# Two token sequences of 256 columns in the place of one of 512, with the adaLN products moved to TensorE

## What is computed

```python
for i in range(DEPTH):                      # h = x, hc = ctx, m / mc = adaln(c) / adaln(c_ctx), 9 rows of 1024 each
    h  = half_ffn(h,  m,  0, g[0], g[1], ffn_w_in[i, 0], ffn_w_out[i, 0])
    hc = half_ffn(hc, mc, 0, g[0], g[1], ffn_w_in[i, 0], ffn_w_out[i, 0])
    u, uc = modulated_norm(h, g[2], m, 3), modulated_norm(hc, g[2], mc, 3)
    y, yc = mixer(u, uc, ..., ctx_out=i < DEPTH - 1)     # x's queries see the keys of both, the context's only its own
    h = half_ffn(gated_residual(h, y, g[3], m, 3, 1.0), m, 6, ...)
    if ctx_out:
        hc = half_ffn(gated_residual(hc, yc, g[3], mc, 3, 1.0), mc, 6, ...)
```

## Time and profile before

| | |
|---|---|
| median of 3 runs | 2817.33 us (2813.98 to 2820.81) |
| span of the profiled execution, first to last instruction | 2814.7 us |
| busy: TensorE / its weight loads | 2602.5 / 2247.8 us |
| busy: VectorE / ScalarE | 1710.1 / 1002.3 us |
| read from HBM | 348.91 MB |
| mean granted TensorE clock | 0.928 of full |

### The profile page before, as it was taken

How to read it: one execution, slowest core, us unless ns; L and a number is a source line. 1 busy time by engine, 2 the same in 40 slices (tenths; PEclk the granted TensorE clock), 3 DMA queues, 4 the chain that set the end, 5 groups by cost and what they waited for, 6 DMA issues and landing times. The chain is left out here.

```text
span 2814.7 us, 39425 instructions
## 1 busy us (share of the span) xinstructions
PE 2602.5 (92%) x14572; PEld 2247.8 (80%) x14572; DVE 1710.1 (61%) x3265; ACT 1002.3 (36%) x1597; POOL 0.8 (0%) x5
## 2 busy tenths in 40 slices
PE   7989988888998999999987899999899999888997
PEld 7989978758997888877855678888688888667997
DVE  3365554446556888435666678873678863656555
ACT  4244442334443222233255332223322223335443
POOL 0000000000000000000000000000000000000000
PEclk9599997758999999998998999999899999989999
DMA  5245452103543554332310135533245532211443
GB/s 212 106 144 185 157 223 84 43 1 134 180 160 131 180 179 150 110 114 88 113 53 1 60 125 176 178 130 103 80 165 179 179 117 92 94 60 61 165 166 118
DMA packets 65732, 351.54 MB, mean 125 GB/s; under 512 B 7376, under 2 KB 10960, under 8 KB 40528
## 3 DMA queue, kind: packets, MB, share of 16 engines
q1 hardware_dynamic: 62272, 341.86, 34.6%
q10 hardware_dynamic: 3344, 8.12, 0.8%
HBM read 348.91 MB, written 1.05 MB: 124 GB/s over the span
## 5 line engine op out<-in xcount | busy, mean ns | idle before, releaser
L309 DVE TENSOR_TENSOR wlo<-raw,whi 128x2048 fp32r<-128x2048 f32 (+1 forms) x282 | 582.2, 2064 | 602.8 <-ACT whi L302 602.0
L314 PE MATMUL bank<-HN_hi,whi 128*128 128x256 f32 (+1 forms) x2976 | 645.1, 342 | 58.7 <-ACT HN_hi L826 31.8
L302 ACT ACTIVATE whi<-raw 128x2048 fp32r<-128x2048 f32 (+1 forms) x282 | 488.7, 1733 | 526.5 <-PE bank L314 508.3
L314 PE MATMUL bank<-HN_hi,wlo 128*128 128x256 f32 (+1 forms) x2976 | 626.6, 335 | 0.0
L314 PE MATMUL bank<-HN_lo,whi 128*128 128x256 f32 (+1 forms) x2976 | 606.3, 334 | 0.0
L314 PEld LDWEIGHTS bank<-HN_hi,whi 128*128 128x128 f32 x2976 | 485.3, 195 | 137.5 <-issue 33.7
L314 PEld LDWEIGHTS bank<-HN_hi,wlo 128*128 128x128 f32 x2976 | 485.6, 194 | 52.5 <-issue 0.5
L314 PEld LDWEIGHTS bank<-HN_lo,whi 128*128 128x128 f32 x2976 | 479.4, 194 | 53.9
L314 PE MATMUL bank<-G_hi,whi 128*128 128x256 f32 (+1 forms) x1056 | 207.4, 345 | 4.4 <-DVE wlo L309 4.4
L314 PE MATMUL bank<-G_lo,whi 128*128 128x256 f32 (+1 forms) x1056 | 198.9, 336 | 0.0
L314 PE MATMUL bank<-G_hi,wlo 128*128 128x256 f32 (+1 forms) x1056 | 198.6, 336 | 0.0
(11 more groups left out here) (223 smaller groups left out, 2086.5 us busy)
## 6 DMA issues: line engine op xcount, KB each, us to landing
raw<-w_main SPq DMA_DIRECT2D x186, 1024.0 KB, 4.8
raw<-w_down SPq DMA_DIRECT2D x96, 704.0 KB, 4.1
half<-w_ada SPq DMA_DIRECT2D x128, 512.0 KB, 4.4
raw<-w_ada SPq DMA_DIRECT2D x8, 1024.0 KB, 4.7
ARENA<-cmp_k_w ACTq DMA_DIRECT2D x1, 2048.0 KB, 11.4
ARENA<-cmp_v_w ACTq DMA_DIRECT2D x1, 2048.0 KB, 18.6
H<-x SPq DMA_DIRECT2D x1, 1024.0 KB, 6.7
H<-x ACTq DMA_DIRECT2D x1, 1024.0 KB, 6.1
```

The source lines that it names most:

```text
L302: NS.activation(WHI[n % 2][:, 0:size], RAW[slot][:, 0:size], ACT.Copy).then_inc(sems["w_hi"], 1)
L309: NV.tensor_tensor(WLO[slot][:, 0:size], RAW[slot][:, 0:size], WHI[n % 2][:, 0:size].bitcast(fp32), SUB)\
L314: return NT.matmul(out[:, 0:N], (WHI[n % 2], WLO[n % SLOTS])[w][:, k * wk + col:k * wk + col + P], x[xp][:, kx, 0:N], start=start, stop=stop)
```

## The change

Nearly all of `build` is rewritten. What it does:

- x and the context have tensors of their own (`Lane`), with 256 columns each. Every weight block of the 117 is loaded, split and multiplied once for x and once for the context.
- A plan of block uses in one order (`take`) replaces the loops; the program is fully unrolled. All weight blocks go through the four `RAW` slots, the 72 of adaLN and the 4 of the NSA compression too. `WHI` has three buffers.
- Three generators are interleaved when the program is written: x's sequence, the context's (`c`), adaLN's (`a`). x's yields `("L", us)` where it expects a wait of that length, `D` ahead of a block and `d` in its middle. In a wait (`fill`) the context gets half blocks at a price of 2.9 us each. Ahead of every second block of x (`pace`) one adaLN block is put in. `want` runs the context in one piece up to its keys and values.
- adaLN on TensorE: the weights are the moving side, 8 float32 matmuls of 256 columns, with 32 stationary columns in turn in four column tiles; then a ScalarE copy, two small matmuls and a VectorE add.
- Silu is formed as tanh on ScalarE and two multiplies on VectorE, over 512 columns (two tiles) at a time.
- The context's FFN is cut in three chunks of hidden features (8, 8, 6 tiles), and its down projection is summed over them in `YC` by VectorE. The context's attention has two banks and one unit in flight.
- The first mixer's parts and `od_in`'s blocks are in another order, so that the rotations, pooling and the compression stand between linear blocks.

By these budgets, counted over the yields of the new text: of the context's 117 blocks 29 are put into x's waits (8 in the NSA attention, 1 in the group norm after it, 5 in the first mixer and the norm after ev_out, 15 in the other norms of x and the tile norm after ga_in). 24 stand in one piece ahead of the first attention, with one norm of the context among them, and 64 ahead of the second, with two. The first 12 adaLN blocks stand in ev_in, 10 of these in a row.

```diff
+def modulation():
+    bank = BANK[5]
+    for b in range(72):
+        yield ("D",)
+        n = take("a", "w_ada", b, BLK, False)
+        landed(n)
+        if on(pe, silu_c if b == 0 else None, free.get(bank.name)):
+            for k in range(KD):
+                g = k % 4
+                mm = NT.matmul(bank[32 * g:32 * g + 32, 0:T], CCOL[:, k, :], RAW[n % SLOTS][:, k * T:(k + 1) * T],
+                               start=k < 4, stop=k >= 4, skip_group_check=True, tile_position=(0, 32 * g))
+            mm.then_inc(sems["block_done"], 1)
+        splits(n)
+        ...
+        if on(act, done(n), picked):
+            NS.activation(ROWS[:, :], bank[:, 0:T], ACT.Copy).then_inc(rows.sem, 1)
+        yield ("L", 0.5)
+        ...
+                mm = NT.matmul(bank[:, T + 2 * m:T + 2 * m + 2], ROWS[:, m * P:(m + 1) * P], vec("pick"), start=True, stop=True)
+def fill(us):
+    credit[0] = min(credit[0] + us, 6.0)
+    ...
+    while credit[0] > 0:
+        if ahead["c"] in ("D", "d"):
+            credit[0] -= 2.9
+            step("c")
+        elif ahead["c"] == "L" and "c" not in late:
+            late.add("c")
+            credit[0] -= 0.3
+            step("c")
+        ...
+def pace(kind):
+    ...
+    if kind == "D":
+        spent[0] += 1
+        if ahead["a"] == "L":
+            step("a")
+        if ahead["a"] == "D" and "a" not in paused and ((0, 1) not in gains_known or spent[0] % 2 == 0):
+            step("a")
+    ...
+    if ahead["c"] == "L":
+        step("c")
+def want(label):
+    while label not in passed:
+        step("c")
+def two_tiles(S, n, dsts, x, ks, start, stop, waits=None, signal=None, tiles=2):
+    landed(n)
+    for m in range(tiles):
+        mm = three(dsts[m], n, m * P, x, ks, start, stop, None if m else waits)
+        ...
+        if m == 0:
+            splits(n)
+        if m == 0 and tiles == 2:
+            opened[0] = S.tag
+            yield ("d",)
+        ...
+def norm(S, post, pre, ready, mod=()):
+    ...
+    if post:
+        yield ("L", 3.0)
+        tot_y = add_up(S, S.YY, sum_y, 0, now(f"{t}_sq_sum"), *ready)
+        ...
+        yield ("L", 1.0)
+        ...
+        yield ("L", 1.5)
+        ...
+    yield ("L", 3.0)
+    rs_h = spread_in(S.SQ[-1], S.wide_h, diag)
+    ...
```

In the context's FFN the last chunk of the down projection ends in `put_out`, which for each of 8 output tiles has 3 operations on ScalarE and 4 on VectorE with one buffer for the squares, and `linear` and `ffn` of the context wait for all 8 feature tiles of its norm:

```diff
+            dst = y if c == 1 else S.TMP[0][:, :]
+            ...
+                NV.tensor_tensor(dst, y, bank[:, :], ADD).then_inc(ev.sem, 1)
+            ...
+            if c == 2:
+                for m in range(2):
+                    held["tmp"] = put_out(S, S.TMP[0][:, m * T:(m + 1) * T], 2 * mp + m, gain, ev)
...
+    x = yield from norm(C, True, pre(C, 0, 1), [now("c_evac")], mods)
+    zk = yield from linear(C, "da_in", [(4 + b, 2 * b) for b in range(4)], KC, ready=x[1])
```

A unit of the context's attention issues its scores, maxima, exps and scalings in one step; the VectorE operations after the exps stand behind them in its queue, ahead of x's:

```diff
+            if on(dve, sc, o):
+                ...
+                NV.tensor_scalar(NEGM, MAXM, -scale, None, MUL).then_inc(ng.sem, 1)
+            if on(act, ng):
+                ...
+            if on(dve, ex):
+                NV.reciprocal(CO, SUM).then_inc(m1.sem, 1)
+                ...
+                NV.scalar_tensor_tensor(PB[:, 0, :], PB[:, 1, :], CO[:, 1:2], PB[:, 0, :], MUL, ADD).then_inc(m4.sem, 1)
+            yield ("L", 1.2)
```

More of the change, by code:

```diff
@@ L52 @@
[L52 to L81, removed]
@@ L84 @@
[L84 to L96, removed]
+SLOTS, HIS = 4, 3
@@ L100 @@
+GU = 22
+PAIRS = KF // 2
+CHUNKS = ((0, 8), (8, 16), (16, 22))
+MAIN, _at = {}, 0
+for _name, _n in [("ev_in", 6), ("ev_out", 4), ("gu0", GU), ("od_in", 14), ("od_out", 4), ("gu1", GU), ("gu2", GU),
+                  ("da_in", 12), ("da_out", 4), ("gu3", GU), ("gu4", GU), ("ga_in", 6), ("ga_out", 4), ("gu5", GU)]:
+    MAIN[_name] = _at
+    _at += _n
 VEC_COLS = {}
@@ L109 @@
 NVEC = _at
[L111 to L116, removed]
-Mark = namedtuple("Mark", "sem n")
+Mark = namedtuple("Mark", "sem n")
+@dataclass
+class Lane:
+    tag: str
+    seq: int
+    H: Any
+    HN: Any
+    Y: Any
+    G: Any
+    TMP: Any
+    SQ: Any
+    DIAG: Any
+    YY: Any
+    GG: Any
+    HG: Any
+    col: int
+    tiles: Any
+    pair: Any
+    sums: Any
+    wide_y: Any
+    wide_h: Any
+    chunked: bool
+    lag: bool
 def build(nc, A, out):
@@ L202, in now @@
                 return Mark(sems[name], count[name])
[L204 to L222, removed]
@@ L700, in add_up @@
+            def add_up(S, buf, bank, at, *ready):
+                total = up(f"{S.tag}_total")
+                if on(pe, *ready, free.get(bank.name)):
+                    for c in range(2):
                         mm = NT.matmul(bank[:, at + c:at + c + 1], buf[:, c * P:(c + 1) * P], ones[:, 0:1], start=True, stop=True)
@@ new lines, in tile_norm @@
+            def tile_norm(S, items, gain, factor, ready, eps, sums, banks, keep=False):
+                n, last = len(items), {}
+                buf = S.TMP[0][:, 0:2 * n]
+                for j, src in enumerate(items):
+                    sq = up("act_step")
+                    b = S.SQ[j % len(S.SQ)]
+                    if on(act, last.get(j - len(S.SQ)), *ready):
+                        NS.activation(b[:, :], src, ACT.Square).then_inc(sq.sem, 1)
+                    if j % 2:
+                        yield ("L", 0.6)
+                    total = up("pe_step")
+                    if on(pe, sq, free.get(sums.name) if j == 0 else None):
+                        for c in range(2):
+                            mm = NT.matmul(sums[:, 2 * j + c:2 * j + c + 1], b[:, c * P:(c + 1) * P], ones[:, 0:1], start=True, stop=True)
```

2433 lines of the change are left out of this document (1257 added, 1176 removed).

## The result

The changed kernel takes **3228.6 us** (median of 4 runs, 3223.56 to 3232.01), the kernel before 2815.7 beside it: a ratio of 1.147, with a 95% interval of 1.145 to 1.150. The forecast was slower by 2%, 2878 us, with 3000 as the upper end. The direction was right, the size was not: 351 us are missing.

What follows compares the result with a forecast made beforehand. TensorE was taken to set the pace where dense, and a chain over all engines in its waits. Nine terms summed to +61 on the 2814.7 us span, 2876, or 2878 with 2.6 outside it; range 2735 to 3000.

Steps and rivals of the forecast that it cites:

- the paragraph on the ring: Weight slots shared with adaLN: landing, copy and remainder take 9.0 us of 13.4, so queueing was priced at nothing.
- Rival C: Weights come late: each of 60 adaLN blocks outside ev_in's row costs 2 us, +120, 2998 us; chance 0.08.
- Narrow columns: Linear blocks and FFNs: 256 columns with doubled weight loads, extra splits hidden where TensorE is dense; -17 us.
- Context in the waits: 29 of the context's 117 blocks go into x's waits at 5.74 us each; -166 us.
- step 3: Context work lengthens x's 8 norms and the tile norm by 6 us each, +54; in the NSA attention nothing.
- step 5: First mixer: old adaLN matmuls go and pooling moves between linear blocks; 64 us becomes 22, -42.
- adaLN on TensorE: 72 adaLN blocks at 1.9 us, plus 1.2 more for each of 10 in a row in ev_in; +149 us.
- rival B: adaLN's column tiles run one after another, a block takes 4.0 us, +151, 3029 us; chance 0.13.
- od_in and NSA: od_in, NSA and smaller stages: the new order hides part of the time over the linear rate; -25 us.
- First attention: Context units delay x's work by 7.2 us a pair, +32; fewer transposes and narrower tile norm return 16; +16.
- The context in one piece: Context's norms stand bare, 32 us for each of 3, and 16 for chunk ends, transposes and key norm; +112.
- Second attention: Of its 77 us, rotations go beside the context's matmuls and the tile norm is narrower; -20 us.

Runs made afterwards that it cites:

- run 5: Changed kernel without adaLN (2895.8 us), with the context doing nothing until x needs its first keys and values: 2952.4 us.
- experiment 6: Changed kernel without adaLN (2895.8 us), with the context's attention standing still while x's first attention runs: 2841.4 us.
- run 8: The first edit (3102 us), with the context beginning only when the first three adaLN rows are there: 3056.0 us.
- the first edit: Changed kernel (3228.6 us), with the split-ahead counting only blocks that are split, so adaLN blocks use up no look-ahead: 3102.2 us.

## Why the prediction was wrong in size

The step that failed is the paragraph on the ring. It set landing, copy and remainder (9.0 us) against 13.4 and called the rest slack, "I price it at nothing". It compared durations and not places in a queue: the remainder was ready to be made long before, but was written behind a step that waits for the end of the block. Its price is 202 us (124 and 78). Rival C named the right sign, waits for wlo over 1 us in the FFNs, at 60 x 2 = 120 us, with 0.08, and had late weights as its cause; 41 waits came, of 3.6 us on average, and behind nearly all of them came the half clock, some 1.8 us each, which no term had.

By the prediction's own steps:

1. **Narrow columns**: right. The rate is 119.8 against 119.6 ns, behind the last adaLN block ScalarE's waits for landings come to 22 us in all, so that the 471.6 MB do not bind there, and in dense stretches the splits were hidden.
2. **Context in the waits**: 28.5 blocks stood there, 29 were taken. But "-166" took them for free outside the norms. For 21 of them run 5 shows 95.5 us of cost in the waits, where step 3 has 30 for its norms and nothing for the rest.
3. **Six us a norm**: about right for three norms (7.4, 5.3, 10). At the one before FFN 4 the norm itself added 9 (FFN 3 and it take 218.5 us, 209 without the context in the table's stages), and the gate and up blocks behind it took 157.3 us with what they waited for, against 137.1 in experiment 6, where the context was at another place. There VectorE first had 16 operations of the context's sums in its queue, and the remainders of two blocks behind them:

```profile
2190.30 0.42 DVE L327 TENSOR_TENSOR sumch<-sumch,tmpc 128x256 f32<-128x256 f32 x1
2190.63 0.42 DVE L329 TENSOR_TENSOR sumcg<-sumcg,tmpc 128x256 f32<-128x256 f32 x1
2190.97 4.49 DVE L204 TENSOR_TENSOR wlo<-raw,whi 128x2048 fp32r<-128x2048 f32 x2
```

   The mixers are the larger miss: 43 us at the start for five blocks, for which step 5 left an unnamed part of 22, and 29.5 around NSA for ten, of which step 3 priced the eight in the attention at nothing because TensorE had time free there.
4. **adaLN on TensorE**: right. 134 us against 149, 1.66 a block against 1.9. The four column tiles run side by side: 8 matmuls of 256 columns in 1.07 us, where the prediction's estimate for one after another is 3.4, which ends rival B. The Trainium skill (TensorE: Matmul & The Clock Gate, Measured speedup vs the span model) gives 2.38 for three tiles; with that estimate 3.4 / 1.07 = 3.2 for four is the same share for each tile. The prediction's own use of the 2.38 was reckoned wrong: 1.43 with its 0.5 and 0.55 makes 2.5 us a block and some 40 us more, not 2.2 and 20. The Trainium skill also says that changing the tiling mode drains TensorE (TensorEngine Tiling (Array Packing), Key Properties): the last linear matmul starts at 288.99 and the first tile at 289.20, 0.21 us where two linear ones are 0.12 apart, so this costs 0.1 us at most on the way in.
5. **First mixer**: right, if the context is out of it: 130.2 against 168.4 is -38, taken as -42.
6. **od_in and NSA**: right, 267.9 against 288.7 is -21, without the context; -25 was for this and smaller stages.
7. **First attention**: +16 was +63 (192 against 129). The 7.2 us a pair (its four terms add up to 7.0) had the legs of VectorE and ScalarE and left out TensorE's own, some 5 us at the half clock, which stand in the same loop; x's maxima, which it counted, lie beside them. Where TensorE's order has the context's scores right behind x's, as in run 8, a pair takes 6.9.
8. **The context in one piece**: right. 175 + 434 us for 88.5 blocks of 5.74 are 101 over the rate, 112 were taken. A norm of the context takes 26.3 us from the start of the last matmul before it to that of the first behind it, not 32:

```profile
1618.99 0.28 PE L225 MATMUL bank<-GC_hi,wlo 128*128 128x256 f32 x1
1628.21 0.99 PE L507 MATMUL bank<-VEC,sumcy 128*128 128x1 f32 x4 [8.94 <-ACT ARC L310]
...
1645.30 0.55 PE L225 MATMUL bank<-HNC_hi,whi 128*128 128x256 f32 x1 [11.21 <-DVE HNC_lo L638]
```

9. **Second attention**: -20 was wrong. 35 us of tile norm and rotations between ga_in and the context's piece stayed bare, with a block and a half of the context in them; with the 53 behind it that is 88, and 79 without the 8.6 us of these, against 77.

Ring and look-ahead 202, attention 47, the mixers some 60 (43 + 29.5 less the two norms counted), step 9 22, the norm before FFN 4 24 (9 + 20 and some tenths, less the six), less 15 and 11 that steps 4 and 8 had too much: 329 of 351. The other 22 I have not placed. The mixers and adaLN's work were measured in kernels without adaLN or its loads, one run each, so the sum takes for granted that these costs add.

## What to carry to other kernels

When work of another kind is put into a numbered stream of blocks, ask what every look-ahead, ring and due time counts, and follow the queue of each engine at that place: a step is late by where it stands, not by what the engine has to do. A gap of 2.7 to 3.8 us on TensorE cost its length here and mostly 1.4 to 2.8 us more at the half clock. Two latency-bound chains written into one order can become one loop: the context's unit added 7 us beside x's unit, 4 where its scores were written right behind x's, and some 2 beside dense work. After taking away the first cause of a wait, look at what other engines now wait for: the second stood right behind it.

## What the runs showed that I had not expected

- The two causes lay one behind the other: with the first edit TensorE's waits for wlo fell from 199 to 70 us, while ScalarE's waits for landings rose from 184 to 523 us.
- The place of one unit's matmuls in TensorE's order decided an attention, with the clock going along: a pair takes 9.9 us at a granted clock of 0.61, or 6.9 at 0.87; a unit of x alone takes 2.85 at 0.95.
- After a wait of 2.7 us behind 1.07 us of adaLN the linear matmuls come 0.21 us apart for 13 to 26 matmuls in most periods and for only two in others; a column-tile group by itself takes 1.07 us at full clock and 1.94 at the half.
